# Last layer's closing norm: the last unit's rows are added by VectorE instead of by products with the identity

## The chip, the cores and the metric

One core of a Trainium2 chip runs the whole program in one launch. The metric is the device time of one execution in microseconds; the kernel before was run three times (median 1253.22 us, lowest 1249.56, highest 1257.2). One more execution was recorded by the hardware profiler, and all rows below are from that one.

## The reference

The reference is a two-layer encoder trunk on 512 tokens of width 1024, float32 throughout. Each layer does a mixer and then a mixture of experts, each followed by a residual sum and a layer norm. Cut to what matters here:

```
def _layer_norm(x, w, b):
    xf = x.astype(jnp.float32)
    mu = jnp.mean(xf, axis=-1, keepdims=True)
    var = jnp.mean(jnp.square(xf - mu), axis=-1, keepdims=True)
    return ((xf - mu) * lax.rsqrt(var + LN_EPS) * w + b).astype(x.dtype)

def reference(...):
    h = x
    for layer in range(DEPTH):                  # DEPTH = 2
        ...                                     # mixer of this layer, first norm
        y = _moe(h, router_w, moe_w_gate[layer], moe_w_up[layer], moe_w_down[layer])
        h = _layer_norm(DN_ALPHA * h + y, ln_w[layer, 1], ln_b[layer, 1])
    return h
```

The mixture picks for each token one group of experts and the two best experts in it; `y` is the sum of the two experts' rows for that token, each times its gate. The change touches only the last line of the second layer: the sum `DN_ALPHA * h + y` and the layer norm over it, whose result is the output.

## The kernel before

The engines have one instruction stream each, written by hand, and they meet on semaphores; there is no scheduler. What an engine does next is always the next instruction in its own stream.

The 512 tokens lie as four tiles of 128 rows, `h[:, t, :]` with 1024 columns, in SBUF for the whole program (`t` is the tile, `L` the layer, 0 or 1). In the expert stage the tokens are packed by expert into units of 128 rows. TensorE runs `gate`, `up` and `down` for one unit after another (L788 and L825). ScalarE copies a unit's result out of PSUM (L1099), and stores it in DRAM (`slot_rows`), from where GpSimd's indirect DMA gathers two rows per token (L2152). VectorE merges these into `h`, which GpSimd has multiplied by `DN_ALPHA` before: two instructions for each tile, `merge(t)`, L1728 and L1730.

The last unit is not sent through DRAM. Its rows stay in SBUF as `y_last`, and for each tile a product with a 128x128 selection matrix (`last_selT`, L899) puts each row at its token, times its gate, straight into the two PSUM banks `2t` and `2t+1`. How these rows come to the merged `h` differs by layer:

- In layer 0, L899 starts its banks from nothing, and VectorE adds PSUM to `h` (L1739).
- In layer 1, TensorE first multiplies the merged `h` by the identity (L894) into the same banks, and L899 accumulates on it. The banks then hold the full sum, and VectorE never adds: `tile_of(3, t)` names `ps` as the source of the norm's statistics and of its centring.

One product of 128x128 by 128x512 in float32 is two matmul rows in the trace, so a tile's two halves are four rows by L894 and four by L899.

The norm of a tile has this chain, on three engines. VectorE: two statistics instructions (L1665), their aggregation (L1667), plus epsilon (L1668). ScalarE: the square root (L1199). VectorE: the reciprocal (L1674), and `centre`, (x - mean) * weight, which writes `h` (L1679). In layer 1, tiles 0 to 2 are finished elsewhere: ScalarE scales the tile by the reciprocal (L1383), GpSimd adds the bias `lnb` (L2190), and SyncE's queue stores it (L525). Tile 3 is scaled and shifted by VectorE in one instruction (L1687), and stored. `done(...)` makes VectorE wait until the instruction given to it has written.

```
            # ScalarE, last layer, for each tile
                norm_std(3, t)
                if t < NT - 1:
                    act.wait_ge(ln_centred, t + 1)
                    nc.scalar.activation(h[:, t, :], h[:, t, :], ACT.Copy, scale=col("rst1", t, 1)).then_inc(ln_scaled, 1)
            # GpSimd, last layer
            for t in range(NT - 1):
                pool.wait_ge(ln_scaled, t + 1)
                pool.tensor_tensor(h[:, t, :], h[:, t, :], lnb, ALU.add).then_inc(ln_done, 1)
```

Of the kernel before, what the change touches and what calls it, by code (L numbers as in the profile page):

```python
# [15 lines left out]
ALU = mybir.AluOpType  # L16
# [6 lines left out]
NT = T // P  # L23
# [103 lines left out]
def encoder_kernel(nc, x, w_in_even, w_out_even, lru_conv_w, lru_conv_b, lru_gate_w, lru_gate_b,  # L127
# [3 lines left out]
    with ExitStack() as ctx:  # L131
        def sb(name, shape, dt=F32):
            return ctx.enter_context(nc.sbuf_tensor(name, shape, dt))

        def sem(name):
            return ctx.enter_context(nc.semaphore(name))


        h = sb("h", [P, NT, D])
# [15 lines left out]
        ident, ones, upper = sq[:, 0, :], sq[:, 1, :], sq[:, 2, :]  # L155
        ps = ctx.enter_context(nc.psum_tensor("ps", [P, 8, 512], F32))
# [170 lines left out]
        h_scaled, merged, summed = sem("h_scaled"), sem("rows_merged"), sem("last_rows_summed")  # L327
# [202 lines left out]
        def _(pe):  # L530
# [109 lines left out]
            for k in range(16):  # L640
                n, zg = k // 4, k % 4
# [97 lines left out]
            def moe(L):  # L739
# [102 lines left out]
                for t in range(NT):  # L842
                    pe.wait_ge(sel_done, L * (NT + 1) + t + 1)
                    for half in range(2):
                        last = pe.matmul(ps[:, 2 + half, :], first_sel[:, t, :], h[:, t, half * 512:(half + 1) * 512],  # L845
                                         start=(t == 0), stop=(t == NT - 1))
# [41 lines left out]
                for t in range(NT):  # L888
                    if t == 1:
                        pe.wait_ge(y_copied[L], copies)  # L890
                    if L == 1:
                        pe.wait_ge(merged, NT + t + 1)
                        for half in range(2):
                            pe.matmul(ps[:, 2 * t + half, :], ident, h[:, t, half * 512:(half + 1) * 512],  # L894
                                      start=True, stop=False)
                    if t == 0:
                        pe.wait_ge(y_copied[L], 2 * NU)
                    for half in range(2):
                        last = pe.matmul(ps[:, 2 * t + half, :], last_selT[:, t * P:(t + 1) * P],  # L899
                                         y_last[:, half * 512:(half + 1) * 512],  # L900
                                         start=(L == 0), stop=True)
                    last.then_inc(summed, 1)


# [37 lines left out]
            spin(1, 6)  # L942
            router(0)
            moe(0)


# [144 lines left out]
            spin(1, 6)  # L1091
            router(1)
            moe(1)


# [291 lines left out]
        def _(dve):  # L1387
            v = nc.vector
            count = [0]

            def done(ins):

                count[0] += 1
                ins.then_inc(dve_order, 1)
                dve.wait_ge(dve_order, count[0])
# [261 lines left out]
            def tile_of(n, t):  # L1657

                halves = h[:, t, :].rearrange("p (a n) -> p a n", a=2)
                return halves, ps[:, 2 * t:2 * t + 2, :] if n == 3 else halves  # L1660

            def statistics(n, t, halves=(0, 1)):
                _, src = tile_of(n, t)
                for half in halves:
                    last = v.bn_stats(col("st", 6 * half, 6), src[:, half, :])  # L1665
                done(last)
                done(v.bn_aggr(col("ag", 2 * t, 2), col("st")))  # L1667
                v.tensor_scalar(col("std", t, 1), col("ag", 2 * t + 1, 1), LN_EPS, None, ALU.add).then_inc(var_done, 1)  # L1668

            def centre(n, t, signal=None):  # L1670
                halves, src = tile_of(n, t)
                if n % 2 or t < NT - 1:
                    dve.wait_ge(std_done, n * NT + t + 1)
                    v.reciprocal(col("rst1", t, 1), col("std", t, 1))  # L1674
                if t == 0:
                    dve.wait_ge(lnp_in, 32 * (n + 1))
                if n % 2 == 0:
                    dve.wait_ge(hT_ps, (n + 1) * 2 * NT + 2 * t + 2)
                ins = v.scalar_tensor_tensor(halves, src, col("ag", 2 * t, 1), lnw.rearrange("p (a n) -> p a n", a=2),  # L1679
                                             ALU.subtract, ALU.mult)  # L1680
                if signal is None:
                    done(ins)
                else:
                    ins.then_inc(signal, 1)

            def shift(t, signal=ln_done):
                v.scalar_tensor_tensor(h[:, t, :], h[:, t, :], col("rst1", t, 1), lnb, ALU.mult, ALU.add  # L1687
                                       ).then_inc(signal, 1)
# [32 lines left out]
            def norm_moe(L):  # L1721

                def merge(t):

                    dve.wait_ge(gathered[t], (L + 1) * 32)
                    if t == 0:
                        dve.wait_ge(h_scaled, L + 1)
                    done(v.scalar_tensor_tensor(h[:, t, :], Yg[L][t // 2][:, 2 * (t % 2), :], gts[:, t, 0:1], h[:, t, :],  # L1728
                                                ALU.mult, ALU.add))
                    v.scalar_tensor_tensor(h[:, t, :], Yg[L][t // 2][:, 2 * (t % 2) + 1, :], gts[:, t, 1:2], h[:, t, :],  # L1730
                                           ALU.mult, ALU.add).then_inc(merged, 1)

                def norm(t):

                    dve.wait_ge(summed, L * NT + t + 1)
                    if L == 0:
                        halves, _ = tile_of(1, t)
                        dve.wait_ge(merged, t + 1)
                        done(v.tensor_tensor(halves, ps[:, 2 * t:2 * t + 2, :], halves, ALU.add))  # L1739
                    statistics(2 * L + 1, t)  # L1740
                    centre(2 * L + 1, t, ln_centred if L == 1 and t < NT - 1 else None)
                    if L == 0:
                        shift(t)
                    elif t == NT - 1:
                        shift(t, ln_centred)

                if L == 0:
                    merge(0)
                    merge(1)
                    norm(0)  # L1750
                    merge(2)
                    merge(3)
                else:
                    for t in range(NT):
                        merge(t)
                    norm(0)
                for t in range(1, NT):
                    norm(t)
# [456 lines left out]
```

## Time and profile before

| what | value |
|---|---|
| runs, median (lowest to highest) | 1253.22 us (1249.56 to 1257.2) |
| the profiled execution's own time | 1250.46 us |
| its span in the trace | 1248.5 us |
| granted TensorE clock, mean of the span | 0.992 of full |
| TensorE busy / VectorE busy | 1205.0 us (97%) / 547.5 us (44%) |
| ScalarE busy / GpSimd busy | 213.7 us (17%) / 172.5 us (14%) |
| last merge of a tile starts (L1730, tile 3) | 1229.51 us |
| last VectorE instruction (L1687, tile 3) | 1244.02 us, for 1.28 us |

Times in the trace are microseconds from the start of the span. Busy time is the sum of an engine's instructions over the whole program; the change lies in the last 25 us of it, and there the shares are others. So the rows below are mostly of that stretch. A row of the timeline gives start, duration, engine, line, operation and tile names, shapes, and in brackets the idle time of the engine ahead of it with what ended it.

### The profile page before, as it was taken

Reading aid. Unit: us, or ns where it says so; the run is one execution under the profiler, and the core shown is the slowest. Engines: PE = TensorE matmul, PEld = TensorE weight load, DVE = VectorE, ACT = ScalarE, POOL = GpSimd, SP = SyncE. Lnnn points to the kernel's source line nnn. Section 1 sums busy time; section 2 is a strip of 40 time slices with the busy share of each in tenths; the row PEclk is TensorE's granted clock in tenths of the full one; section 3 lists DMA queues with packets and bytes.
Section 4 is the critical chain, followed back from the end, with each engine's and each line's share of the span. In section 5 each row is a group of like instructions: output and inputs, shape, how many; then the busy total and the mean of one; then the engine's idle time right before and its main releaser. Section 6 shows DMA issues by size and latency. Waiting matters only on the chain.

```text
span 1248.5 us, 14147 instructions
## 1 busy us (share of the span) xinstructions
PE 1205.0 (97%) x5567; PEld 579.3 (46%) x5567; DVE 547.5 (44%) x1058; ACT 213.7 (17%) x336; POOL 172.5 (14%) x132
## 2 busy tenths in 40 slices
PE   8999999999999998899999999999899899999987
PEld 4784464543333333444555555555454433333332
DVE  1885892663211112800655565556625723111107
ACT  0017400210000001112122212221112100000002
POOL 0002100003000002000222232223300022000013
PEclk9999999999999999999999999999999899999998
DMA  9900096389999999453222022200055899999994
GB/s 344 359 1 0 30 375 265 124 334 397 428 427 427 426 427 382 155 128 135 67 68 68 7 62 68 67 0 1 0 213 225 319 394 414 427 425 428 426 425 177
DMA packets 78547, 294.74 MB, mean 236 GB/s; under 512 B 6580, under 2 KB 46360, under 8 KB 65688
## 3 DMA queue, kind: packets, MB, share of 16 engines
q1 hardware_dynamic: 67904, 266.22, 54.2%
q0 software_dynamic: 4896, 17.83, 3.7%
q10 hardware_dynamic: 5688, 9.85, 2.1%
q8 instruction: 44, 0.72, 0.2%
q14 instruction: 15, 0.12, 0.0%
HBM read 271.34 MB, written 22.54 MB: 235 GB/s over the span
## 4 chain that ended last, share of the span: by engine, by line
PE 85%; DVE 7%; DMA 6%; issue 1%; ACT 1%; DVEq 0%; SPq 0%
PE ps L788 20%; PE ps L969 15%; PE ps L825 9%; PE ps L694 8%; PE ps L577 4%; PE ps L991 4%; PE ps L574 4%; PE ps L956 4%; DMA W<-moe_w_down 3%; DMA S<-moe_w_down 3%; PE ps L562 2%; PE ps L1021 2%; PE ps L845 2%; PE ps L744 1%; PE ps L665 1%; DVE S L2036 1%
## 5 line engine op out<-in xcount | busy, mean ns | idle before, releaser
L788 PE MATMUL ps<-W,S 128*64 128x512 f32 (+1 forms) x1200 | 272.6, 594 | 2.5 <-ACT S L1099 1.5
L969 PE MATMUL ps<-hT,W 128*128 128x512 f32 x512 | 232.6, 593 | 0.7 <-ACT W L1099 0.7
L788 PEld LDWEIGHTS ps<-W,S 128*64 128x64 f32 (+1 forms) x1200 | 81.6, 123 | 133.0 <-issue 129.6
L788 PE MATMUL ps<-S 128*32 128x512 f32 (+1 forms) x592 | 140.3, 593 | 0.5 <-DVE S L1950 0.5
L969 PEld LDWEIGHTS ps<-hT,W 128*128 128x128 f32 x512 | 93.0, 191 | 90.2 <-issue 88.4
L825 PE MATMUL ps<-W,hT 128*64 128x512 f32 (+1 forms) x512 | 114.6, 600 | 5.0 <-DMA W<-moe_w_down 2.2
L2174 POOL TENSOR_TENSOR W<-S,sq 128x256 f32<-128x256 f32 x64 | 73.5, 1149 | 159.3 <-PE ps L991 115.5
L1099 ACT ACTIVATE hT<-ps 128x512 f32<-128x512 f32 x68 | 39.1, 597 | 319.5 <-PE ps L825 235.4
L2132 POOL DMA_INDIRECT S<-token_rows,row_at x18 | 17.4, 968 | 507.7 <-PE ps L744 288.1
L825 PE MATMUL ps<-S,hT 128*32 128x512 f32 (+1 forms) x384 | 84.9, 594 | 1.0 <-DVE hT L1977 1.0
L2078 DVE TENSOR_TENSOR S<-S 128x512 f32<-128x512 f32 x64 | 47.8, 747 | 68.1 <-PE ps L991 56.3
L991 PEld LDWEIGHTS ps<-S,W 128*128 128x128 f32 x448 | 61.3, 192 | 30.1 <-issue 30.1
L1968 DVE TENSOR_TENSOR hT<-hT,ps 128x512 f32<-128x512 f32 x20 | 13.7, 685 | 127.8 <-ACT hT L1213 127.8
L991 PE MATMUL ps<-S,W 128*128 128x128 f32 x448 | 63.6, 286 | 1.4 <-issue 0.8
L1977 DVE COPY hT<-ps 128x512 f32<-128x512 f32 x20 | 13.8, 690 | 110.7 <-PE ps L814 110.7
L788 PEld LDWEIGHTS ps<-S 128*32 128x32 f32 (+1 forms) x592 | 40.5, 118 | 45.5 <-issue 44.4
L1973 DVE TENSOR_TENSOR hT<-hT,ps 128x512 f32<-128x512 f32 x20 | 13.8, 688 | 108.6 <-PE ps L788 101.4
L825 PEld LDWEIGHTS ps<-W,hT 128*64 128x64 f32 (+1 forms) x512 | 34.2, 125 | 55.3 <-issue 54.2
L1099 ACT ACTIVATE W<-ps 128x512 f32<-128x512 f32 x56 | 32.9, 603 | 153.3 <-PE ps L988 39.5
L694 PE MATMUL ps<-S 128*128 128x512 f32 x128 | 57.7, 594 | 1.0 <-DVE S L2016 1.0
L956 PE MATMUL ps<-W,hT 128*128 128x512 f32 x128 | 56.0, 594 | 1.7 <-DMA W<-w_in_odd 1.0
L694 PE MATMUL ps<-W,hT 128*128 128x512 f32 x128 | 55.9, 593 | 0.0
(305 smaller groups left out, 1407.0 us busy)
## 6 DMA issues: line engine op xcount, KB each, us to landing
W<-moe_w_gate SPq DMA_DIRECT2D x22, 2048.0 KB, 17.0
W<-moe_w_up SPq DMA_DIRECT2D x20, 2048.0 KB, 19.9
W<-moe_w_down SPq DMA_DIRECT2D x20, 2048.0 KB, 22.7
S<-moe_w_down SPq DMA_DIRECT2D x12, 2048.0 KB, 21.9
S<-moe_w_up SPq DMA_DIRECT2D x10, 2048.0 KB, 20.1
S<-moe_w_gate SPq DMA_DIRECT2D x8, 2048.0 KB, 17.0
W<-w_in_odd SPq DMA_DIRECT2D x32, 512.0 KB, 6.5
slot_rows<-hT ACTq DMA_DIRECT2D x18, 512.0 KB, 11.0
```

Of the source, the lines that this page charges most:

```text
L562: last = pe.matmul(ps[:, 4 + n, :], hT[:, c, n * P:(n + 1) * P], w_grp[0][:, c, :], start=(c == 0), stop=(c == ND - 1))
L574: last = pe.matmul(bank[:, k, :], wf[:, c, m * P:(m + 1) * P], xf[:, c, :], start=(c == 0 and k == 0), stop=(c == 3 and k == 1))
L577: last = pe.matmul(bank, xf[:, c, b * P:(b + 1) * P], wf[:, c, :], start=(c == 0), stop=(c == 3))
L694: last = pe.matmul(ps[:, k, :], srcT[:, c, t * P:(t + 1) * P], w[:, c, half * 512:(half + 1) * 512], start=(start and c == tiles[0]), stop ...
L788: last = pe.matmul(ps[a:a + n, bank, :], xgT[:, c, a:a + n], home(kind, p)[:, c, :], start=(c == 0), stop=(c == ND - 1))
L825: last = pe.matmul(ps[a:a + n, 2 + half, :], hidT[:, c, a:a + n], home(DOWN, p)[:, c, half * 512:(half + 1) * 512], start=(c == 0), stop=( ...
L956: last = pe.matmul(ps[:, k, :], hT[:, c, t * P:(t + 1) * P], w_v1[c // 4][:, c % 4, (k % 2) * 512:(k % 2 + 1) * 512], start=(c == 0), stop ...
L969: last = pe.matmul(ps[:, f % 2, :], ring[slot][:, f, c, :], hT[:, c, :], start=(c == 0), stop=(c == ND - 1))
L991: last = pe.matmul(o, km[level % 2][:, c * P:(c + 1) * P], mixed(Q2, s, c * P, P), start=True, stop=True)
L1099: return nc.scalar.activation(o, i, ACT.Copy)
L2078: v.tensor_tensor(q, q, view(src, at + 1, [[2, n], [step - 1, 2], [0, s]]), ALU.mult).then_inc(updated, 1)
L2174: pool.tensor_tensor(view(km[level % 2], s, [[4 * s, m], [s, 2], [1, s]]), view(K2, s, [[4 * s, m], [T + s, 2], [1, s]]), view(ones, 0, [[ ...
```

## The change

In layer 1 the identity products are taken out, and L899 starts its banks itself, as in layer 0. VectorE adds the banks to the merged `h` of each tile, and the statistics and the centring read `h` in SBUF and no longer PSUM.

```diff
@@ TensorE, end of moe(L)
                 for t in range(NT):
                     if t == 1:
                         pe.wait_ge(y_copied[L], copies)
-                    if L == 1:
-                        pe.wait_ge(merged, NT + t + 1)
-                        for half in range(2):
-                            pe.matmul(ps[:, 2 * t + half, :], ident, h[:, t, half * 512:(half + 1) * 512],
-                                      start=True, stop=False)
                     if t == 0:
                         pe.wait_ge(y_copied[L], 2 * NU)
                     for half in range(2):
                         last = pe.matmul(ps[:, 2 * t + half, :], last_selT[:, t * P:(t + 1) * P],
                                          y_last[:, half * 512:(half + 1) * 512],
-                                         start=(L == 0), stop=True)
+                                         start=True, stop=True)
                     last.then_inc(summed, 1)
@@ VectorE, tile_of(n, t)
-                return halves, ps[:, 2 * t:2 * t + 2, :] if n == 3 else halves
+                return halves, halves
@@ VectorE, norm(t) in norm_moe(L)
                     dve.wait_ge(summed, L * NT + t + 1)
-                    if L == 0:
-                        halves, _ = tile_of(1, t)
-                        dve.wait_ge(merged, t + 1)
-                        done(v.tensor_tensor(halves, ps[:, 2 * t:2 * t + 2, :], halves, ALU.add))
+                    halves, _ = tile_of(1, t)
+                    dve.wait_ge(merged, L * NT + t + 1)
+                    done(v.tensor_tensor(halves, ps[:, 2 * t:2 * t + 2, :], halves, ALU.add))
                     statistics(2 * L + 1, t)
                     centre(2 * L + 1, t, ln_centred if L == 1 and t < NT - 1 else None)
```

TensorE's stream at the very end of the program, before (the number behind x counts products in a row):

```order
L894 MATMUL ps<-h,sq 128x512 x2
L899 MATMUL ps<-S 128x512 x2
L894 MATMUL ps<-h,sq 128x512 x2
L899 MATMUL ps<-S 128x512 x2
L894 MATMUL ps<-h,sq 128x512 x2
L899 MATMUL ps<-S 128x512 x2
L894 MATMUL ps<-h,sq 128x512 x2
L899 MATMUL ps<-S 128x512 x2
```

And in the changed kernel, where the selection products stand at L894:

```order
L894 MATMUL ps<-S 128x512 x8
```

The eight products with the identity are gone, and the eight of the selection follow each other.

VectorE's stream from the last merge to the centring of tile 1, before (`S` holds gathered rows and the norm's weight, `sm` the small columns of statistics):

```order
L1730 SCALAR_TENSOR_TENSOR h<-S,gts,h 128x1024
L1665 BN_STATS sm<-ps 128x6 x2
L1667 BN_AGGR sm<-sm 128x2
L1668 TENSOR_SCALAR sm<-sm 128x1
L1674 RECIPROCAL sm<-sm 128x1
L1679 SCALAR_TENSOR_TENSOR h<-ps,sm,S 128x1024
L1665 BN_STATS sm<-ps 128x6 x2
L1667 BN_AGGR sm<-sm 128x2
L1668 TENSOR_SCALAR sm<-sm 128x1
L1674 RECIPROCAL sm<-sm 128x1
L1679 SCALAR_TENSOR_TENSOR h<-ps,sm,S 128x1024
```

The same stretch in the changed kernel, whose lines are five or six lower:

```order
L1725 SCALAR_TENSOR_TENSOR h<-S,gts,h 128x1024
L1733 TENSOR_TENSOR h<-ps,h 128x1024
L1660 BN_STATS sm<-h 128x6 x2
L1662 BN_AGGR sm<-sm 128x2
L1663 TENSOR_SCALAR sm<-sm 128x1
L1669 RECIPROCAL sm<-sm 128x1
L1674 SCALAR_TENSOR_TENSOR h<-h,sm,S 128x1024
L1733 TENSOR_TENSOR h<-ps,h 128x1024
L1660 BN_STATS sm<-h 128x6 x2
L1662 BN_AGGR sm<-sm 128x2
L1663 TENSOR_SCALAR sm<-sm 128x1
L1669 RECIPROCAL sm<-sm 128x1
```

Each of the four tiles gets one more instruction, the 128x1024 addition; the statistics read `h` where they read `ps`, and the centring reads `h` and `S` where it read `ps` and `S`. The streams of ScalarE, GpSimd and SyncE are the same in both.

## Rows read from the trace of the kernel before

**Rows 1.** The page's busy times: engine, us, share, instructions.

```profile
PE 1205.0 (97%) x5567; PEld 579.3 (46%) x5567; DVE 547.5 (44%) x1058; ACT 213.7 (17%) x336; POOL 172.5 (14%) x132
```

**Rows 2.** Chain that ended last, at the end: start, us, what.

```profile
1226.67 1.91 PE ps L894 x4
1228.59 1.72 PE ps L899 x4
...
1238.89 1.73 PE ps L899 x4
...
1240.64 1.31 DVE sm L1665 x2
```

**Rows 3.** Timeline of VectorE, last merge to the end.

```profile
1229.51 1.28 DVE L1730 SCALAR_TENSOR_TENSOR h<-S,gts,h 128x1024 f32<-128x1024 f32 x1
1230.71 1.29 DVE L1665 BATCH_NORM_STATS2 sm<-ps 128x6 f32<-128x512 f32 x2
1232.78 1.27 DVE L1679 SCALAR_TENSOR_TENSOR h<-ps,sm,S 128x1024 f32<-128x1024 f32 x1
1233.96 1.29 DVE L1665 BATCH_NORM_STATS2 sm<-ps 128x6 f32<-128x512 f32 x2
...
1236.04 1.26 DVE L1679 SCALAR_TENSOR_TENSOR h<-ps,sm,S 128x1024 f32<-128x1024 f32 x1
1237.22 1.29 DVE L1665 BATCH_NORM_STATS2 sm<-ps 128x6 f32<-128x512 f32 x2
...
1240.64 1.30 DVE L1665 BATCH_NORM_STATS2 sm<-ps 128x6 f32<-128x512 f32 x2
...
1244.02 1.28 DVE L1687 SCALAR_TENSOR_TENSOR h<-h,sm,S 128x1024 f32<-128x1024 f32 x1
```

**Rows 4.** Timeline of VectorE in layer 0, tile 1 of the same norm.

```profile
509.53 1.22 DVE L1739 TENSOR_TENSOR h<-ps,h 128x1024 f32<-128x1024 f32 x1
510.78 1.29 DVE L1665 BATCH_NORM_STATS2 sm<-h 128x6 f32<-128x512 f32 x2
```

**Rows 5.** Instructions of L1665 and L1679 by source: ns min/median/max, first and last start.

```profile
L1665 DVE BATCH_NORM_STATS2 sm<-h x22: 676/694/696, 200.5 to 968.4; 128x6 f32<-128x512 f32 x22
L1665 DVE BATCH_NORM_STATS2 sm<-ps x8: 682/686/698, 1230.7 to 1241.3; 128x6 f32<-128x512 f32 x8
L1679 DVE SCALAR_TENSOR_TENSOR h<-h,sm,S x12: 1266/1274/1286, 221.3 to 980.5; 128x1024 f32<-128x1024 f32 x12
L1679 DVE SCALAR_TENSOR_TENSOR h<-ps,sm,S x4: 1265/1266/1266, 1232.8 to 1242.7; 128x1024 f32<-128x1024 f32 x4
```

**Rows 6.** Timeline of TensorE and ScalarE around the last copies, layer 1, then layer 0.

```profile
1226.71 0.60 ACT L1099 ACTIVATE S<-ps 128x512 f32<-128x512 f32 x1 [2.84 <-PE ps L825]
...
495.93 0.60 ACT L1099 ACTIVATE S<-ps 128x512 f32<-128x512 f32 x1 [2.84 <-PE ps L825]
...
498.67 1.23 DVE L1739 TENSOR_TENSOR h<-ps,h 128x1024 f32<-128x1024 f32 x1 [1.85 <-PE ps L899]
```

**Rows 7.** Timeline of ScalarE and GpSimd in the closing norm.

```profile
1234.08 1.15 ACT L1383 ACTIVATE h<-h,sm 128x1024 f32<-128x1024 f32 x1 [1.41 <-DVE h L1679]
1235.31 2.36 POOL L2190 TENSOR_TENSOR h<-h,S 128x1024 f32<-128x1024 f32 x1 [14.23 <-ACT h L1383]
```

**Rows 8.** Timeline of VectorE and GpSimd, two earlier stretches where both read SBUF.

```profile
124.95 4.53 POOL L2127 TENSOR_TENSOR S<-S 128x2048 f32<-128x2048 f32 x1 [22.06 <-DVE W L1567]
...
126.19 5.44 DVE L1436 TENSOR_TENSOR W<-W,h 128x2048 f32<-128x2048 f32 x1
131.56 2.28 DVE L1550 TENSOR_TENSOR W<-W 128x2048 f32<-128x2048 f32 x1
...
722.08 1.61 POOL L2165 COPY W<-W 128x512 f32 x1
...
723.15 1.23 DVE L2037 TENSOR_TENSOR W<-W,S 128x512 f32<-128x512 f32 x1
724.41 0.69 DVE L2058 TENSOR_TENSOR S<-S 128x512 f32<-128x512 f32 x1
```

## The prediction

> **What bounds the kernel now.** I read four views, from coarse to fine. The page's busy times say that TensorE works 97% of the span and VectorE 44% [rows 1], which makes taking products off TensorE and giving work to VectorE look like a good trade. That share is a mean over the whole program, and the change lies in its last 22 us, so the next view is the chain of waits at the end. It too names TensorE: from 1226.67 to 1240.62 us it is eight pieces in turn, four by L894 (the identity) and four by L899 (the selection), about 1.72 us each, and only then VectorE [rows 2]. A chain names the releaser that came last, though, not by how much. For that I read VectorE's own timeline. Its last merge starts at 1229.51, and the statistics of tile 0 start at 1230.71, directly behind it. The statistics of tiles 1 and 2 start at 1233.96 and 1237.22, a cadence of 3.25 to 3.26 us, and each begins 1.18 us after the centring that stands ahead of it began (1232.78 to 1233.96, 1236.04 to 1237.22), which is how closely two VectorE instructions follow each other here [rows 3]. So VectorE did not wait for TensorE on those tiles. Only on tile 3 it did: by the cadence it would have started at 1237.22 + 3.26 = 1240.48 and it started at 1240.64, 0.16 us late [rows 3]. TensorE needs 3.44 us for a tile (two pieces of 1.72) and VectorE 3.26; they run neck and neck, and VectorE's row of norms is itself the bound but for 0.16 us.
>
> **What the removed products can give.** Without L894, TensorE goes to L899 of tile 0 as soon as ScalarE has copied the second half of the last unit, 1226.71 + 0.60 = 1227.31 us [rows 6]. In layer 0, where the program already has this form, the copy's end at 495.93 + 0.60 = 496.53 is followed by VectorE's add at 498.67, 2.14 us later [rows 6]. The same distance here gives 1229.45 for tile 0 and then 1.72 us for each further tile, the last at about 1234.6. VectorE cannot use tile 0 before 1230.71, since the merges of all four tiles stand ahead of it in its stream, and these wait for gathered rows and not for TensorE. So 1.26 us of slack is there at tile 0, more on each later tile, and TensorE leaves the path. The gain is the 0.16 us of tile 3 and nothing else. The 6.9 us of identity products (four times 1.72) ran beside VectorE.
>
> **What the added instruction costs.** The 128x1024 addition PSUM + `h` is in the trace, in layer 0: start 509.53, and the statistics behind it, which wait for its result through `done`, start at 510.78. That is 1.25 us of VectorE's time per tile [rows 4], on the path on all four tiles since nothing else fills VectorE's stream: 4 x 1.25 = 5.00 us. The other edit on VectorE is the source. Statistics from `h` have a median of 694 ns, from PSUM 686; the centring has 1274 from `h` and 1266 from PSUM [rows 5]. By these medians a tile would cost 0.02 us more (two statistics and a centring), but the layer-0 rows of a pair last 1.29 us just as the layer-1 ones [rows 3, 4]. I take nothing for it, and keep 0.1 us for the range.
>
> Sum so far: 5.00 - 0.16 = 4.84 us. The new cadence of a tile is 3.26 + 1.25 = 4.51 us.
>
> **A second cost: the centring against GpSimd's bias add.** GpSimd adds the bias of tile t while VectorE is at tile t+1. The first of these starts at 1235.31, which is 2.53 us after the centring of tile 0 started (1232.78), and takes 2.36 us [rows 3, 7]. The centring of tile 1 starts at 1236.04 in the middle of it and takes 1.26 us, undisturbed [rows 3]. But that centring reads one tile from SBUF (the weight) and one from PSUM; in the changed kernel it reads two from SBUF. What VectorE does with two SBUF operands beside a GpSimd instruction that reads SBUF is in the trace elsewhere. L1436 starts at 126.19, while GpSimd is busy from 124.95 to 129.48, and lasts 5.44 us, where the 128x2048 instruction behind it takes 2.28: it ends at 131.63, 2.15 us after GpSimd's end. L2037 starts at 723.15, GpSimd is busy until 723.69, and it lasts 1.23 instead of the 0.69 of its neighbour, ending at 724.38, 0.69 after GpSimd's end [rows 8]. So such an instruction is held until GpSimd's is over, and then needs its full time, less 0 to 0.13 us. The Trainium skill says the same in "SBUF — State Buffer", section "Who interferes with whom": a VectorE instruction with two SBUF inputs contends with a GpSimd instruction that reads SBUF, the second to start is held completely, and one with at most one SBUF input isn't touched. Both pairs above and the centring of tile 1 agree with it (5.44 and 1.23 us, against 1.26 undisturbed).
>
> Does the centring meet it? With cadence 4.51 us, the centring of tile t+1 starts 4.51 us after that of tile t. GpSimd's add is busy from 2.53 to 2.53 + 2.35 = 4.88 us after it. They overlap in their last 0.37 us; less the 0.13 us that the first pair shows, 0.24 us. Since the centring of tile t+1 then shifts, and with it its own bias add, the same meeting recurs for tiles 2 and 3: 3 x 0.24 = 0.72 us, at most 3 x 0.37 = 1.11, and nothing if the end of GpSimd's row is drawn 0.4 us late. A long hold is excluded, because at 4.51 us most of GpSimd's add is over. The addition itself has one SBUF operand, and so have the statistics; like the centring of tile 1 they should pass. Tile 3's last instruction (L1687) has two SBUF operands, but comes 1.30 us behind a centring that already waited, when GpSimd has finished its third and last add.
>
> The total is 4.84 + 0.72 = 5.56 us. What lies behind VectorE's last instruction (the store of tile 3, 1248.5 - 1245.30 = 3.2 us) stays. The span goes from 1248.5 to 1254.1 us, the profiled execution from 1250.46 to 1256.0. That execution lay 2.8 us below the median of the three runs; the median goes from 1253.22 to 1258.8.
>
> **Rivals.**
> 1. *TensorE is the bound, as the chain says* (faster). Then the end loses the four identity pieces, 6.9 us, and gets back one addition, 1.25, for the last tile: 5.6 us less, 1247.6 us. For it speaks the chain [rows 2] and TensorE's 97%. Against it: it needs VectorE to have idled ahead of each tile's statistics, and it did so for 0.16 us in all. It would decide if VectorE's four norms could be done in 10.7 us instead of 4 x 3.26 = 13.0. Chance 0.03.
> 2. *The statistics are held by GpSimd too* (clearly slower). Now they read `h` in SBUF, and I have no row of them beside GpSimd. GpSimd's add starts 2.53 us after the centring, the second statistics instruction of the next tile at 1.18 + 1.25 + 0.65 = 3.08 us after it; held until 4.75, it would be 1.67 us late, three times: 5.0 us in place of the 0.72. That is 4.84 + 5.0 = 9.8, a median of 1263.0. Against it: the centring with one SBUF operand passes freely [rows 3]. Chance 0.07.
> 3. *The adds disappear* (no change). It would need gaps in VectorE's stream that the add can fill. Between 1230.7 and the end the only ones are the some 0.3 us in each tile in which it waits for the square root, and the add stands ahead of them in order and can't move in. Or the merges end earlier without TensorE reading `h`; nothing shows that this slows them now, their rows last 1.28 us. 1253 to 1254 us. Chance 0.07.
> 4. *The forecast without the hold* is part of my case: 1253.22 + 4.84 = 1258.1 us; with the largest hold, 1253.22 + 5.95 = 1259.2.
>
> TensorE's clock is no rival. Even at half of full speed the selection products of tile 0 would take twice 1.72 us from 1227.45, to 1230.9, about when VectorE arrives.
>
> **From cases to numbers.** The forecast has 0.83. Its own range from the terms is 1258.1 to 1259.2; the three runs of the same program lie 7.6 us apart, so a median of runs can be some 3 us off, and I widen to 1255 to 1262.5. That leaves out rival 1 and nearly all of rivals 2 and 3 (about 0.17). About 0.5% of the time, 6.3 us, is what a measurement can tell from no change. My 5.6 us lies just inside it, on the slower side: a measured difference over 6.3 us needs only 0.7 us of scatter on top. Of the forecast's 0.83 I give 0.31 to beyond the bound and 0.51 within, 0.01 to a scatter the other way. With rival 2 slower is 0.38, with rival 3 within is 0.58, with rival 1 faster is 0.04.
>
> **What would show it.** In the changed trace: the addition of tile 0 starts at 1230.7, right behind the last merge, with no wait for TensorE on any tile; starts of the additions 4.5 us apart, 4.75 with the hold; the rows of the additions last 1.22 us; the centrings of tiles 1 to 3 read 1.5 us, that of tile 0 1.27; GpSimd's adds stay at 2.35; L899's eight products end before 1235; the chain's end is VectorE alone from the merges on. I am wrong if an addition waits for TensorE, if the statistics' rows grow over 1.35 us while GpSimd works, or if the time moves while VectorE's last instruction still ends near 1245.

## The result

| | before | after |
|---|---|---|
| median of 15 runs (lowest to highest) | 1253.21 us (1249.56 to 1257.2) | 1257.23 us (1253.0 to 1260.77) |
| profiled execution: own time, span | 1250.46, 1248.5 us | 1260.77, 1258.9 us |
| granted TensorE clock over the span | 0.992 | 0.983 |

The ratio of the times is 1.0035, 95% interval 1.0023 to 1.0047: the change costs 4.4 us (2.9 to 5.9), clear of noise and under the bound of 0.5%. The forecast was 5.6 us. The two profiled executions are 10.4 us apart in span, and nearly half of that is not the change: the last unit's down products (L825) start at 1218.26 us before and at 1223.06 us after, 4.8 us later, at a place where both programs are still the same. Over the twelve profiled executions of this document they start anywhere from 1216.21 to 1223.06 us, in no order by kernel. So I measure the tail from there. From the start of those products to the start of VectorE's last instruction it is 1244.02 - 1218.26 = 25.76 us before and 1254.57 - 1223.06 = 31.51 us after. The row of L825 in the kernel before:

```profile
1218.26 8.41 PE L825 MATMUL ps<-W,hT 128*64 128x512 f32 x32 [2.18 <-DMA W<-moe_w_down]
```

The lower mean clock of the changed kernel is in part only its longer end: from 1250 to 1258 us the granted clock is 0.50 while TensorE has nothing to do.

The page's busy times for the changed kernel, in the columns of [rows 1]:

```profile
PE 1202.9 (96%) x5551; PEld 576.5 (46%) x5551; DVE 552.6 (44%) x1062; ACT 213.7 (17%) x336; POOL 172.6 (14%) x132
```

Sixteen TensorE rows are gone and four of VectorE are new. The chain of waits at the end of the changed kernel (start, us, what), which answers to [rows 2]:

```profile
1223.06 10.06 PE ps L825 x32
1233.12 0.02 issue
1233.14 0.61 ACT S L1094
1233.75 0.14 issue
1233.88 1.97 PE ps L894 x4
1235.85 0.02 issue
1235.88 1.24 DVE h L1733
1237.11 0.02 issue
1237.13 1.30 DVE sm L1660 x2
```

From 1235.88 us on the chain stays with VectorE, save for the square roots. That much was forecast. What was not is the way into it: it comes from L825, the copy and the first selection products, not from the merges, and L825 took 10.06 us. VectorE's timeline, changed kernel, answering to [rows 3]:

```profile
1233.96 1.28 DVE L1725 SCALAR_TENSOR_TENSOR h<-S,gts,h 128x1024 f32<-128x1024 f32 x1
1235.88 1.23 DVE L1733 TENSOR_TENSOR h<-ps,h 128x1024 f32<-128x1024 f32 x1 [0.63 <-PE ps L894]
1237.13 1.29 DVE L1660 BATCH_NORM_STATS2 sm<-h 128x6 f32<-128x512 f32 x2
...
1239.20 1.27 DVE L1674 SCALAR_TENSOR_TENSOR h<-h,sm,S 128x1024 f32<-128x1024 f32 x1
1240.39 1.22 DVE L1733 TENSOR_TENSOR h<-ps,h 128x1024 f32<-128x1024 f32 x1
...
1243.71 1.45 DVE L1674 SCALAR_TENSOR_TENSOR h<-h,sm,S 128x1024 f32<-128x1024 f32 x1
1245.09 1.21 DVE L1733 TENSOR_TENSOR h<-ps,h 128x1024 f32<-128x1024 f32 x1
...
1253.09 1.44 DVE L1674 SCALAR_TENSOR_TENSOR h<-h,sm,S 128x1024 f32<-128x1024 f32 x1
1254.57 1.28 DVE L1682 SCALAR_TENSOR_TENSOR h<-h,sm,S 128x1024 f32<-128x1024 f32 x1
```

Three things are to be seen. The additions take 1.21 to 1.23 us and stand 4.51 us apart from tile 0 to 1, then 4.70 and 4.68. The centring of tile 0 takes 1.27 us and those behind it 1.45, 1.45 and 1.44. And ahead of the first addition VectorE idled 0.63 us for TensorE, where the forecast had TensorE done 1.26 us early. GpSimd's first bias add, same kernel, for the 1.45:

```profile
1241.74 2.34 POOL L2184 TENSOR_TENSOR h<-h,S 128x1024 f32<-128x1024 f32 x1 [15.95 <-ACT h L1378]
```

It ends at 1244.08 us, and the centring that started at 1243.71 ends at 1245.16, 1.08 us after it.

### The profile page after: what moved, and what is told of

Its sections match the earlier page's. It is cut to its first block, busy times and chain, and to the rows that moved or that the text cites. A ratio compares the mean times of both kernels' runs of the same rounds, so it can differ in the third digit from the quotient of the medians.

```text
span 1258.9 us, 14122 instructions
## 1 busy us (share of the span) xinstructions
PE 1202.9 (96%) x5551; PEld 576.5 (46%) x5551; DVE 552.6 (44%) x1062; ACT 213.7 (17%) x336; POOL 172.6 (14%) x132
## 4 chain that ended last, share of the span: by engine, by line
PE 81%; DVE 8%; DMA 8%; issue 1%; ACT 1%; SPq 0%; DVEq 0%
PE ps L788 19%; PE ps L964 15%; PE ps L825 9%; PE ps L694 8%; PE ps L986 4%; PE ps L577 4%; PE ps L574 4%; PE ps L951 4%; DMA W<-moe_w_down 3%; DMA S<-moe_w_down 3%; PE ps L1016 2%; DMA W<-moe_w_up 2%; PE ps L562 2%; PE ps L845 2%; PE ps L744 1%; PE ps L665 1%
## 5 line engine op out<-in xcount | busy, mean ns | idle before, releaser
L825 PE MATMUL ps<-W,hT 128*64 128x512 f32 (+1 forms) x512 | 119.2, 613 | 4.9 <-issue 2.2
L825 PE MATMUL ps<-S,hT 128*32 128x512 f32 (+1 forms) x384 | 87.9, 603 | 1.0 <-DVE hT L1971 1.0
L825 PEld LDWEIGHTS ps<-W,hT 128*64 128x64 f32 (+1 forms) x512 | 35.2, 127 | 58.8 <-issue 57.8
```

The lines of the kernel that those rows point to most:

```text
L825: last = pe.matmul(ps[a:a + n, 2 + half, :], hidT[:, c, a:a + n], home(DOWN, p)[:, c, half * 512:(half + 1) * 512], start=(c == 0), stop=( ...
```

## The experiments

The questions, in order: what makes the late centrings longer; what the addition and the removal are each worth; and why TensorE was late.

### The changed kernel again

> The changed kernel once more, for another reading of its tail. Both theories agree on VectorE: additions 4.5 us apart from tile 0 to 1, then 4.7 us, centrings of tiles 1 to 3 of about 1.45 us. Theory A (how late TensorE ends the last unit's down products decides what the change costs, and that varies with the granted clock): from the end of L825 to the start of VectorE's last instruction 21.4 us where L825 takes about 10 us, and the addition of tile 0 has waited for TensorE; where L825 takes under 8.6 us the last instruction starts 19.9 us after the start of the last merge (L1725), with no wait. Rival B (TensorE is always done in time, as the prediction had it): no wait ahead of the first addition, whatever L825 takes.

Ratio 1.0037 (1.0021 to 1.0053). TensorE's last down products, then VectorE's first addition and its last instruction:

```profile
1221.01 9.99 PE L825 MATMUL ps<-W,hT 128*64 128x512 f32 x32 [2.15 <-DMA W<-moe_w_down]
...
1233.77 1.23 DVE L1733 TENSOR_TENSOR h<-ps,h 128x1024 f32<-128x1024 f32 x1 [0.56 <-PE ps L894]
...
1252.45 1.28 DVE L1682 SCALAR_TENSOR_TENSOR h<-h,sm,S 128x1024 f32<-128x1024 f32 x1
```

L825 ends at 1231.00, and the last instruction starts 21.45 us later, as after 1223.06 + 10.06 = 1233.12 us in the first profile of the changed kernel: theory A, not B.

### The sum written back to PSUM

```diff
-                return halves, halves
+                return halves, ps[:, 2 * t:2 * t + 2, :] if n == 3 else halves
...
-                    done(v.tensor_tensor(halves, ps[:, 2 * t:2 * t + 2, :], halves, ALU.add))
+                    total = ps[:, 2 * t:2 * t + 2, :] if L == 1 else halves
+                    done(v.tensor_tensor(total, ps[:, 2 * t:2 * t + 2, :], halves, ALU.add))
```

> The changed kernel, but in the last layer VectorE writes the sum back into PSUM, and statistics and centring read it there, so that no instruction of tiles 0 to 2's norm has two SBUF tensor operands. Theory H (the 0.18 us by which the centrings of tiles 1 to 3 are longer is GpSimd's hold on a VectorE instruction with two SBUF operands): all four centrings take 1.27 us, additions 4.5 us apart on every tile, about 0.5 us less than the changed kernel, ratio to the kernel before about 1.003. Rival (centring from SBUF just takes longer here, or the store of tile t disturbs it): 1.45 us stays. If writing PSUM from VectorE costs more than writing SBUF, the addition's row shows it.

Ratio 1.0041 (1.0026 to 1.0055), which can't tell 0.5 us. The trace can. VectorE around tile 1, with the sum in PSUM:

```profile
1237.93 1.22 DVE L1734 TENSOR_TENSOR ps<-ps,h 128x1024 f32<-128x1024 f32 x1
1239.19 1.30 DVE L1660 BATCH_NORM_STATS2 sm<-ps 128x6 f32<-128x512 f32 x2
...
1241.27 1.26 DVE L1674 SCALAR_TENSOR_TENSOR h<-ps,sm,S 128x1024 f32<-128x1024 f32 x1
1242.45 1.22 DVE L1734 TENSOR_TENSOR ps<-ps,h 128x1024 f32<-128x1024 f32 x1
```

The addition costs the same into PSUM, the cadence is 4.51 to 4.52 us on every tile, and the centring is 1.26 us where GpSimd is busy (its add started at 1239.28). The whole row of norms, from the last merge's start to the last instruction's, is 1251.60 - 1232.21 = 19.39 us, 0.5 us less than the 19.89 of the changed kernel when that doesn't wait for TensorE (below). Theory H stands; its price is three times 0.18 us.

### A long GpSimd instruction, with and without two SBUF operands

The same edit in the changed kernel and in the one just above. The extra sums read only the bias and are used nowhere. Each of the two kernels was executed once (1265.69 and 1259.05 us), so I read their traces and not their times.

```diff
             for t in range(NT - 1):
                 pool.wait_ge(ln_scaled, t + 1)
+                pool.wait_ge(pool_order, 3 + t)
+                pool.tensor_tensor(scratch[:, 0:2048].rearrange("p (a n) -> p a n", a=2),
+                                   view(lnb, 0, [[0, 2], [1, D]]), view(lnb, 0, [[0, 2], [1, D]]), ALU.add).then_inc(pool_order, 1)
```

> The changed kernel, with one more GpSimd instruction ahead of each bias add of tiles 0 to 2, a sum of 128x2048 that reads SBUF and writes scratch (4.5 us by an earlier row). Theory H: the centring of tile 1 starts about 4.5 us after that of tile 0, is held until GpSimd's long instruction ends, about 7 us after it, and reads 3.5 to 3.8 us; the end comes several us later. The additions and the statistics, with one SBUF operand, keep 1.22 and 1.29 us though GpSimd works all through them. Rival (no hold): the centring stays at 1.3 to 1.45 us. Rival 2 of the prediction (one SBUF operand is held too): the statistics grow.

> The sum in PSUM as in the second kernel of this set, with the long GpSimd instruction of the third. Theory H: all centrings 1.27 us and additions 4.5 us apart, although GpSimd reads SBUF through all of them; only the last instruction of tile 3, which reads h and the bias from SBUF, can be held. The span may still grow, since GpSimd's own three times 6.9 us end later than VectorE. Rival (long GpSimd work slows any VectorE instruction): the centrings grow here as well.

GpSimd, then VectorE, changed kernel with the long instruction:

```profile
1238.88 3.60 POOL L2185 TENSOR_TENSOR hT<-S 128x2048 f32<-128x2048 f32 x1 [15.82 <-ACT h L1378]
1242.44 3.34 POOL L2187 TENSOR_TENSOR h<-h,S 128x1024 f32<-128x1024 f32 x1
...
1240.86 2.71 DVE L1674 SCALAR_TENSOR_TENSOR h<-h,sm,S 128x1024 f32<-128x1024 f32 x1
1243.49 1.21 DVE L1733 TENSOR_TENSOR h<-ps,h 128x1024 f32<-128x1024 f32 x1
1244.74 1.29 DVE L1660 BATCH_NORM_STATS2 sm<-h 128x6 f32<-128x512 f32 x2
1246.81 3.62 DVE L1674 SCALAR_TENSOR_TENSOR h<-h,sm,S 128x1024 f32<-128x1024 f32 x1
```

The centring of tile 1 is held until GpSimd ends at 1242.48 and finishes 1.09 us later; GpSimd's next instruction, 3.34 us and not 2.34, is held by it in turn. The centrings of tiles 2 and 3 take 3.62 and 3.61 us. The additions and the statistics between them, with one SBUF operand each, keep 1.21 and 1.29 us though GpSimd works without a pause. So rival 2 of the prediction is out. The size on tile 1 was misjudged (3.5 to 3.8 us expected, 2.71 measured), mostly since GpSimd's long instruction took 3.6 us and not 4.5.

With the sum in PSUM, the centring of tile 1 under the same long instruction, and the last instruction, which reads `h` and the bias:

```profile
1234.22 3.60 POOL L2186 TENSOR_TENSOR hT<-S 128x2048 f32<-128x2048 f32 x1 [15.13 <-ACT h L1378]
...
1236.21 1.26 DVE L1674 SCALAR_TENSOR_TENSOR h<-ps,sm,S 128x1024 f32<-128x1024 f32 x1
...
1246.55 4.08 DVE L1682 SCALAR_TENSOR_TENSOR h<-h,sm,S 128x1024 f32<-128x1024 f32 x1
```

1.26 us in the middle of GpSimd's 3.6, and 4.08 us for the one instruction that has two SBUF operands. That is the hold, switched off and on by the operand's place alone.

### The kernel before again

> The kernel before once more, ratio 1. For the tail: theory A gives the start of VectorE's last instruction (L1687) as the later of two, 14.4 us after the start of the last merge (L1730) or 17.35 us after the end of L825. Where L825 takes about 10 us, VectorE should wait for TensorE on tiles 0 to 3 and the second bound hold by some 1.5 us. Rival B (VectorE's 3.26 us per tile is the bound in every execution): the first bound holds always.

Ratio 0.9992 (0.9978 to 1.0007). The same place in this execution of the kernel before:

```profile
1220.35 8.73 PE L825 MATMUL ps<-W,hT 128*64 128x512 f32 x32 [2.21 <-DMA W<-moe_w_down]
...
1231.12 1.28 DVE L1730 SCALAR_TENSOR_TENSOR h<-S,gts,h 128x1024 f32<-128x1024 f32 x1
1232.75 1.30 DVE L1665 BATCH_NORM_STATS2 sm<-ps 128x6 f32<-128x512 f32 x2 [0.35 <-PE ps L899]
...
1246.43 1.28 DVE L1687 SCALAR_TENSOR_TENSOR h<-h,sm,S 128x1024 f32<-128x1024 f32 x1
```

Here VectorE does wait for TensorE, at tile 0 already, and its tiles go at TensorE's 3.43 us. The last instruction starts at 1229.08 + 17.35 = 1246.43 us, to the digit what theory A gives; by VectorE's own pace it would have been 1231.12 + 14.4 = 1245.5.

### Products in the wait, in both kernels

```diff
                 turn_hidden(LAST)
+                if L == 1:
+                    pe.wait_ge(side_copied, 3 * L + 3)
+                    for n in range(3):
+                        pe.matmul(ps[:, 7, 0:3 * P], ident, sq[:].rearrange("p a n -> p (a n)"), start=True, stop=True)
                 down(LAST)
```

> The kernel before, with three products of 128x384 of constants into a free PSUM bank, issued by TensorE while it waits for the last unit's down weights. Nothing else is changed; the products' results are used nowhere. Theory A: the clock stays at 2.4 GHz over the wait, L825's last 32 rows take about 7.1 us and not 8.4 to 10, TensorE ends early, and the tail is set by VectorE alone, 14.4 us after the last merge starts; against the kernel before it saves 0.1 to 1.8 us, depending on how long the low clock would have lasted. If the products overrun the wait, up to 1 us is lost. Rival: the clock falls all the same, nothing changes.

> The changed kernel with the same three products. Theory A: no wait for TensorE ahead of the first addition, last instruction 19.9 us after the start of the last merge, and the full cost of the change against the sixth kernel: 5.4 to 5.6 us (ratio to that one 1.0044), where it is 4.1 us when TensorE ends late. Rival B: the cost is the same 5.5 us with or without the products, so both kernels move by the same amount.

First TensorE ahead of the last unit in the kernel before with the products. In the windows further down the columns are PE, PEld, DVE, ACT and POOL busy us and rows, granted clock, DMA share and GB/s.

```profile
1218.05 0.75 PE L814 MATMUL ps<-sq,hT 128*128 128x128 f32 x4 [0.84 <-DVE hT L1977]
1218.64 2.10 PE L879 MATMUL ps<-sq 128*128 128x384 f32 x6
1220.97 7.09 PE L825 MATMUL ps<-W,hT 128*64 128x512 f32 x32 [0.23 <-issue]
```

The changed kernel with the products, L825, the first addition and VectorE's last instruction:

```profile
1219.23 7.09 PE L825 MATMUL ps<-W,hT 128*64 128x512 f32 x32 [0.41 <-issue]
...
1231.28 1.22 DVE L1737 TENSOR_TENSOR h<-ps,h 128x1024 f32<-128x1024 f32 x1
...
1249.97 1.28 DVE L1686 SCALAR_TENSOR_TENSOR h<-h,sm,S 128x1024 f32<-128x1024 f32 x1
```

The granted clock over L825: kernel before with the products, kernel before again, changed kernel.

```profile
1220.90:1228.00 7.10, 7.03 (x33) 2.65 (x33) 5.00 (x5) 0.60 (x1) 3.52 (x3) 1.00 1.00 385
```

```profile
1220.30:1229.00 8.70, 8.65 (x32) 2.80 (x32) 6.69 (x6) 0.60 (x1) 1.76 (x2) 0.80 0.78 311
```

```profile
1223.00:1233.00 10.00, 9.94 (x32) 3.14 (x32) 7.83 (x7) 0.60 (x1) 2.18 (x3) 0.70 0.77 307
```

The same 32 rows take 7.09 us at clock 1.00, 8.73 at 0.80 and 10.05 at 0.70: part of them runs at 1.2 and not 2.4 GHz, behind a wait of some 2.2 us. It is the first part: in the changed kernel run again, L825 starts at 1221.01 us, and the clock is 0.50 from 1221 to 1226 us and 1.00 from 1227 to 1231. With the products in that wait the clock stayed up in both kernels; no addition or statistics waits for TensorE, and the last instruction starts 14.33 and 19.89 us after the last merge's start, where 14.4 and 19.9 were expected. VectorE's last instruction starts 1246.15 - 1220.97 = 25.18 us after L825's start in the one and 1249.97 - 1219.23 = 30.74 us in the other, so the change costs 5.56 us there. The measured ratios to the kernel before are 0.9992 (0.9977 to 1.0007) and 1.0049 (1.0030 to 1.0067), 7 us apart by the ratios, 5.6 by the medians (1251.23 and 1256.85); the intervals are too wide to tell 5.6 from 4.4. That the cost rises is shown in the traces and not in the times. As an improvement of the kernel before the products are not proven either: the gain is inside the interval, and the unchanged kernel run again gave the same 0.9992.

### The edit on tile 3 alone

```diff
-                    if L == 1:
+                    if L == 1 and t < NT - 1:
                         pe.wait_ge(merged, NT + t + 1)
...
-                                         start=(L == 0), stop=True)
+                                         start=(L == 0 or t == NT - 1), stop=True)
...
-                return halves, ps[:, 2 * t:2 * t + 2, :] if n == 3 else halves
+                return halves, ps[:, 2 * t:2 * t + 2, :] if n == 3 and t < NT - 1 else halves
...
-                    if L == 0:
+                    if L == 0 or t == NT - 1:
                         halves, _ = tile_of(1, t)
-                        dve.wait_ge(merged, t + 1)
+                        dve.wait_ge(merged, L * NT + t + 1)
```

> The kernel before, with the edit made on tile 3 alone: no identity products for it, VectorE adds it from PSUM and norms it from h. VectorE pays one addition of 1.25 us and meets GpSimd's bias add of tile 2 with a centring that has two SBUF operands; it starts 4.5 us after the one before and should be held about 0.2 us. TensorE ends 1.72 us earlier. If VectorE is the bound: 1.25 - 0.16 + 0.2 = 1.3 us slower. If TensorE had been (L825 of about 10 us): the wait for tile 3 goes, but those for tiles 0 to 2 stay, so 17.35 us after the end of L825 becomes about 18.7 minus at most 0.5, about 1.0 us slower. If the chain of waits were to be taken at its word (TensorE the bound): 0.5 us faster.

Ratio 1.0010 (0.9997 to 1.0024). L825 took 9.96 us here, and the last instruction started 1250.28 - 1231.67 = 18.61 us after its end, 1.26 more than the 17.35 of the kernel before, where about 1.0 was expected for an L825 of that length: of the wait for TensorE that went with tile 3, the 0.17 us of one tile was to be had, not up to 0.5. VectorE waited 1.44 us for TensorE at tile 0, and the centring of tile 3 took 1.45 us. The reading by the chain (0.5 us faster) is out, plainly by the trace and just so by the times.

### The removal alone, the addition alone

```diff
-                    if L == 1:
-                        pe.wait_ge(merged, NT + t + 1)
-                        for half in range(2):
-                            pe.matmul(ps[:, 2 * t + half, :], ident, h[:, t, half * 512:(half + 1) * 512],
-                                      start=True, stop=False)
...
-                                         start=(L == 0), stop=True)
+                                         start=True, stop=True)
```

> The kernel before with the identity products taken out and nothing put in their place: the merged rows are left out of the last norm, which reads the selection products alone from PSUM. It prices what the removal gives. Theory A: the last VectorE instruction starts at the later of 14.4 us after the start of the last merge and 16.1 us after the end of L825 (2.76 to the first statistics, 3 x 3.26 + 3.38 from there). With L825 at about 10 us and the last merge 10.9 us after its start: 26.1 us after the start of L825, against 27.35 in the kernel before, 1.2 us gained; with L825 at 8.4 us 0.2 to 0.5. On average about 0.8 us, ratio 0.9994. Rival B (the forecast's gain of 0.16 us, always): ratio 1.000 and no wait for TensorE. Rival 1 of the prediction (TensorE is the bound throughout): 6.9 us gained, ratio 0.9945.

This kernel leaves the merged rows out of its result. Ratio 0.9994 (0.9982 to 1.0005), so at most 2.3 us and not 6.9. The times can't tell the 0.8 us of theory A from the forecast's 0.16. In its profile the clock happened not to fall (L825 7.09 us behind a wait of 2.17), so the 1.2 us of a late TensorE could not show; the last instruction came 14.33 us after the last merge's start, with no wait, as theory A says for that case.

```diff
                         done(v.tensor_tensor(halves, ps[:, 2 * t:2 * t + 2, :], halves, ALU.add))
+                    else:
+                        done(v.tensor_tensor(scratch[:, 0:D].rearrange("p (a n) -> p a n", a=2),
+                                             ps[:, 2 * t:2 * t + 2, :], tile_of(1, t)[0], ALU.add))
```

> The kernel before with the identity products kept and an addition of the same form and size put into VectorE's stream ahead of each tile's statistics, its sum written to scratch and used nowhere; statistics and centring still read PSUM. It prices the addition alone, without the two SBUF operands. Theory: additions 4.5 us apart on every tile, all centrings 1.27 us; the first addition starts at the later of 1.2 us after the last merge's start and 3.7 us after the end of L825; the last instruction 18.2 us after the first addition. With L825 at 10 us: 31.9 us after its start, 4.6 us more than the kernel before; at 8.4 us: 30.4, also 4.6. Ratio about 1.0037. If the addition could hide in VectorE's gaps, its share would be less.

Ratio 1.0048 (1.0028 to 1.0069). The first addition:

```profile
1232.78 1.23 DVE L1741 TENSOR_TENSOR hT<-ps,h 128x1024 f32<-128x1024 f32 x1 [0.42 <-PE ps L899]
```

L825 ended at 1220.32 + 8.78 = 1229.10, 3.68 us before it; the last instruction starts at 1250.94, 18.16 us after it. From the start of L825 that is 30.62 us, against 8.78 + 17.35 = 26.13, worked out for the kernel before with an L825 as long: 4.5 us for four additions (5.0 us), less the waits for TensorE that they fill. Expected were 4.6.

## Why the forecast held, and where it was off

The median of the changed kernel, 1257.23 us, lies in the stated range of 1255 to 1262.5, and below the narrower one that the terms alone gave, 1258.1 to 1259.2. The interval of the times, 2.9 to 5.9 us, holds the forecast of 5.6, so that it was too high is read from the traces. Of its three terms the additions came out at the forecast 1.25 us of VectorE's time each, and the two that did not (the hold, the removal) both made it too high, so it was not saved by errors that cancel. But one of the prediction's own signs of being wrong did appear: the first addition waited 0.63 us for TensorE.

**The bound.** Right in direction: VectorE's row of norms sets the end and TensorE's products run beside it. "they run neck and neck, and VectorE's row of norms is itself the bound but for 0.16 us" was true of the one execution that I had, and so was the 1.26 us of slack at tile 0. In the second execution of the kernel before, TensorE was the bound on every tile.

**The addition.** 1.25 us per tile was forecast; 4.51 - 3.25 = 1.26 measured. From one tile to the next nothing of it hides (4.50 to 4.52 us apart in the kernel with the addition alone); only waits for TensorE, which the forecast had at 0.16 us, can take some of it in.

**The hold.** 3 x 0.24 = 0.72 us forecast, 3 x 0.18 = 0.54 measured: the held instruction ends 1.08 us after GpSimd, 0.19 us earlier than its full 1.27, where I had taken 0.13 from [rows 8]. The mechanism is shown by switching it on and off. It is in the kernel before too, which the prediction passed over: where VectorE did not wait for TensorE (products in the wait, removal alone) its last instruction took 1.40 us, not 1.28, and ended 1.08 to 1.09 us after GpSimd's third bias add. Counted to the end of that instruction and not to its start, the cost with the products in the wait is 5.44 us and not 5.56.

**The step that failed** is the one that priced the removal: "So 1.26 us of slack is there at tile 0, more on each later tile, and TensorE leaves the path. The gain is the 0.16 us of tile 3 and nothing else." The term is mis-sized. The forecast took 0.16 us off the additions and the hold. By the traces it should have been about 1.0 us on average, from nothing where L825 takes 7.1 us to 1.4 where it takes 10: the removal lets VectorE start its norms sooner, and the additions fill waits for TensorE that the kernel before has (with the products kept, four of them cost 4.5 and not 5.0 us).

With it fell "TensorE's clock is no rival". I looked for a low clock at the selection products only, and took L825's 8.4 us as given. But 8.41 us is 1.32 more than the 7.09 of the same rows at full clock: some of them ran at 1.2 GHz already, and how many do changes from execution to execution.

The tail can be written down as two lines fitted to the traces. Let D be what L825 takes, counted from its start, with the last merge starting 10.9 us after it (10.75 to 11.25 wherever TensorE waited for the down weights or had the products in that wait):

- before: the last instruction starts at the later of 10.9 + 14.36 = 25.3 and D + 17.35;
- after: at the later of 10.9 + 19.89 = 30.8 and D + 21.45.

The 17.35 comes from the first row of the table and the 21.45 from the fourth; 14.36 is added up from rows of the first profile (1.20 + 3 x 3.26 + 3.38), and 19.89 is read from the last row, so those three rows had to agree. The second, third and fifth test the lines; the last does so in part, since 19.9 was expected for it before it ran.

| profile | D | last instruction, measured | by the two lines, with its own last merge |
|---|---|---|---|
| before | 8.41 | 25.76 | 25.76 |
| before, again | 8.73 | 26.08 | 26.08 |
| before, products in the wait | 7.09 | 25.18 | 25.21 |
| after | 10.05 | 31.51 | 31.50 |
| after, again | 9.99 | 31.44 | 31.44 |
| after, products in the wait | 7.09 | 30.74 | 30.74 |

By these lines the change costs 5.5 us at D = 7.1, 5.0 at 8.4, 4.7 at 8.7 and 4.1 at 10; the last is the least tested, since no profile of the unchanged kernel before had a D near 10 (the kernel with the edit on tile 3 had, and VectorE waited 1.44 us there). The nine profiles in which TensorE waited some 2.2 us for the last down weights and had nothing to do in it show D = 7.09, 8.41, 8.73, 8.78, 8.78, 9.96, 9.99, 10.05 and 10.07; the mean of the cost over them is 4.6 us, or 0.36%, and the runs gave 0.35 and 0.37%. That mean assumes that D does not depend on the kernel. Both profiles of the kernel before had a D under 8.8 and both of the changed kernel one near 10, but the kernels that share their TensorE instructions do not part that way: with the identity products (on three tiles at least) 8.41, 8.73, 8.78 and 9.96, without them 7.09, 8.78, 9.99, 10.05 and 10.07. The mean is worked out and not measured; no kernel was made in which D was held high in both, and the gain of the removal behind a late TensorE was never seen by itself.

**The rivals.** TensorE as the bound throughout is out, by the removal alone and by tile 3 alone. The statistics held by GpSimd are out, by the long instruction. The additions disappearing is out. (The 10.7 us in rival 1 follows from no row: with the end 5.6 us earlier, VectorE's row of norms would have had to shrink from 13.3 to 7.7 us, so the rival was further off than stated.) All of them, like the forecast, gave one fixed number; what they lacked was a quantity that varies.

## What to carry to other kernels

When two engines end a stage within a few tenths of a microsecond of each other, the busy shares and the chain name one of them, and a change priced on that one alone will be off by what the other's start varies from one execution to the next; write both bounds and ask what moves each. Before work is moved to VectorE, look at what its instructions read: an operand that came from PSUM and now comes from SBUF can put it behind GpSimd. And a comparison of two profiled executions should start at the last place where both programs are the same: here 4.8 of the 10.4 us between them had nothing to do with the change.

## What was unexpected in the hardware

The clock behind one and the same wait. TensorE waits 2.15 to 2.21 us ahead of the last down products in nine of the twelve profiles (in six of them the profile names the weights' DMA, in three nothing), and then the same 32 rows take anything from 7.09 to 10.07 us; in one of nine the clock did not fall, in four the rows took 2.9 to 3.0 us more. Why it differs is open. The Trainium skill says in "TensorE: Matmul & The Clock Gate", Part 1, of a kernel's start, that the number of matmuls run at the low clock differs between runs of one kernel. These traces show the like behind a wait, if less within one kernel (8.41 and 8.73 us, 10.05 and 9.99) than over kernels that are the same up to there. With three products of 128x384 in the wait the rows took 7.09 us both times, and so they did in the kernel with the sum in PSUM, where the wait happened to be 0.98 us; with one in nine at 7.09 us without any help, that is an indication and not a proof.

The hold works both ways. GpSimd's bias add, 2.34 us alone, took 3.34 us when VectorE's centring with two SBUF operands was waiting when its turn came. And VectorE writes a 128x1024 sum into PSUM in 1.22 us, as fast as into SBUF, so in the trace keeping the sum there avoids the hold at no price of its own; the times (1.0041 against 1.0035 and 1.0037) don't show the gain.
